# A chunked scan whose first chunks are loaded and weighed during the attention stage before it, with six state carries moved from VectorE to GpSimd

## Chip, cores and metric

One core of a Trainium2 chip runs the whole kernel as one program. The metric is device time in microseconds (us), the median of several runs. The engines are PE (TensorE), DVE (VectorE), ACT (ScalarE), POOL (GpSimd) and SP (SyncE, which here only issues DMAs). Each works through its own list of instructions in order, and they meet at semaphores.

## What is computed

One encoder layer over two request groups with shared weights, a prompt of 1024 tokens and a sample of 512: a projection, differential attention, a bidirectional Mamba-2 scan, a gated merge, routed experts, an embedding and a norm. The change lies at the seam of the attention and the scan. The scan, for one direction (it runs a second time over the flipped sequence):

```python
a = dtr * A.reshape(G, R)
acum = jnp.cumsum(a, axis=2)
xdt = xr * dtr[..., None]
...
decay_s = jnp.exp(acum[:, :, -1:] - acum)
states = jnp.einsum('bcjgn,bcjgrp->bcgrpn', Br, xdt * decay_s[..., None])
...
prev = jnp.einsum('bkcgr,bcgrpn->bkgrpn', Dm, states)
y_off = jnp.einsum('bkign,bkgrpn->bkigrp', Cr, prev) * jnp.exp(acum)[..., None]
return (y_diag + y_off).reshape(b, L, SSM_HEADS, P)
```

`states` is what one chunk of 128 tokens adds to the state, and `prev` is the state that a chunk starts from, carried over all chunks before it.

## The kernel before

The kernel is a row of stages, one function each. A stage opens a block in which every engine has its program, and the next stage's block opens when all engines have left the one before. `attend` is followed by `scan_ssm`, then `merge_branches`.

**attend** goes through 48 units (4 heads, 12 tiles of 128 queries). DVE's last work in it is `a` of the last unit (L931). POOL stores the output of a head, the last one by L862, and waits for that store to land before it leaves. SP loads the biases of the last head (L838) and then has nothing left to issue.

**scan_ssm** works on 12 chunks of 128 tokens, 0 to 7 the prompt's and 8 to 11 the sample's, in two phases.

In the first phase the chunks go upward, and each chunk c passes through four engines:
- SP loads `x_in` (a ring of four buffers) from `xb_d`: chunks 0 to 3 at the start (L1050, L1054), each later one when the states of chunk c-4 are made (L1062). Behind chunk 4's load SP waits for the flag `laid`, issues the four loads of `bst` (L1068), and only then loads chunk 5.
- DVE weighs: two TENSOR_TENSOR of 128x1024 multiply `x_in` with the broadcast `wgt` into one of two `wide` buffers (L1120, in `weigh`). From chunk 2 on it waits until the states of chunk c-2 have been made from that buffer.
- PE makes the states of both directions in PSUM (L1304), in one of two sets of banks, so it waits for the copies of chunk c-2.
- ACT copies them out: the forward half to `prev[c + 1]` (L1245), the backward half to `prev[c - 1]` (L1247).

Then the forward carry of a chunk, two TENSOR_TENSOR of 64x1024 (`carry`, L1039 and L1040): `step_ = prev[c] * rate`, `prev[c + 1] += step_`. DVE does them for chunks 1 to 6, 9 and 10, each behind the weighing of the second next chunk (`carry_on`). Beside this come fills: DVE clears four ends of `prev` (L1108), ACT clears `bst` and `mov` (L1214, L1215) before its first copy, and between copies it lays ones, head rows, sides and skips (L1221, L1227, L1232, L1238). The flag `laid` rises when the first head rows are laid.

In the second phase the chunks go downward, n = 0 for chunk 11 to n = 11 for chunk 0. PE waits for all copies, then for the count of carries, and multiplies (L1317, L1329, L1352); ACT takes exponentials (L1263, L1267, L1271), DVE multiplies and gates (L1156, L1160, L1151, L1171), and POOL adds up the squares of a finished chunk in a tree of three additions (L1203, L1204, L1207). The backward carries stay on DVE in this phase.

Of the kernel before, what the change touches and what calls it, by code (L numbers as in the profile page):

```python
# [18 lines left out]
P = 128  # L19
D = 1024  # L20
# [758 lines left out]
def attend(nc, qkT_d, v_d, line_d, ident, raw, q_hi, q_lo, k_hi, k_lo, bias0, lam, o_ssq, o_d, g_out):  # L779
# [14 lines left out]
    with ExitStack() as ctx:  # L794
        sb = lambda n, s, d=F32: ctx.enter_context(nc.sbuf_tensor("at_" + n, s, d))
        sem = stage_semaphores(nc, ctx, "at_")
        idn = sb("idn", [P, P])
# [12 lines left out]
        consts_in = sem("consts_in")  # L810
# [93 lines left out]
        @block.vector  # L904
        def _(dve):
            for k in range(NU + 1):
                if k < NU:
                    head, g0, b, L = UNITS[k]
                    hs = head % 2
                    if k % PER == 0 and head:  # L910
                        dve.wait_ge(bias_landed[hs], 32 * (P // REP) * ((head + 1) // 2))
                    at = (T1 - P) - b * P
                    if k >= 2:
                        dve.wait_ge(mixed, k - 1)
                    dve.wait_ge(sc_full, k + 1)
# [66 lines left out]
def scan_ssm(nc, xb_d, bcT_d, wgt, etot, zgT_d, d_skip, tri_d, ident, decay_d, yT_d, var_d):  # L982
# [14 lines left out]
    with ExitStack() as ctx:  # L997
        sb = lambda n, s, d=F32: ctx.enter_context(nc.sbuf_tensor("sc_" + n, s, d))
        sem = stage_semaphores(nc, ctx, "sc_")
        tri, ones, idn, idr = sb("tri", [P, 4, P]), sb("ones", [P, P]), sb("idn", [P, P]), sb("idr", [P, P], F32R)  # L1000
        far, pick = sb("far", [P, 2, P], F32R), sb("pick", [P, H])
        dsk = sb("dsk", [P, H])
        x_in = sb("x_in", [P, XR, D + P])
        wide = sb("wide", [P, 2, H, P])
# [31 lines left out]
        def carry(eng, chain, d, c, to):  # L1036
# [8 lines left out]
        carried_f = [c for c in range(NC) if c not in FIRST and c not in LAST]  # L1045
# [3 lines left out]
        def _(sp):  # L1049
            sp.dma_start(x_in[:, 0], xb_d[0][:, 0:D + P]).then_inc(x_landed[0], 16)  # L1050
            for out, src in ((idn[:], ident), (dsk[:], d_skip.to_broadcast([P, H])), (tri[:], tri_d)):
                sp.dma_start(out, src).then_inc(consts_in, 16)
            for c in range(1, XR):
                sp.dma_start(x_in[:, c], xb_d[c][:, 0:D + P]).then_inc(x_landed[c], 16)  # L1054
# [49 lines left out]
        def _(dve):  # L1104
            dve.memset(ones[:], 1.0)
            for d, zeros in ((0, FIRST), (1, LAST)):
                for c in zeros:
                    last = dve.memset(prev[side(d), c], 0.0)  # L1108
            last.then_inc(ones_set, 1)
            r = Chain(dve, carry_step)  # L1110

            def weigh(chunk):
                r, s = chunk % XR, chunk % 2
                dve.wait_ge(x_landed[r], 16 * (chunk // XR + 1))
                if chunk >= 2:
                    dve.wait_ge(st_full, chunk - 1)
                xw = flat(wide[:, s])
                for d in range(2):
                    w = wgt[:, chunk, d * H:(d + 1) * H].unsqueeze(2).to_broadcast([P, H, SP_])
                    last = dve.tensor_tensor(heads(xw[:, d * D:(d + 1) * D]), heads(x_in[:, r, 0:D]), w, ALU.mult)  # L1120
                last.then_inc(spread, 1)

            weigh(0)
            dve.wait_ge(consts_in, 48)
# [4 lines left out]
            weigh(1)  # L1129
# [47 lines left out]
            for n in range(NC):  # L1177
# [7 lines left out]
                if c in carried_b:  # L1185
                    carry(dve, r, 1, c, c - 1)
# [12 lines left out]
        def _(pool):  # L1199
            t = Chain(pool, tree)  # L1200
# [10 lines left out]
        def _(act):  # L1211
            act.preload_act_table(ACT.Exp)
            act.wait_ge(ones_set, 1)
            act.activation(bst[:].rearrange("p c d j -> p (c d j)"), ones[:, 0:1].to_broadcast([P, NC * 2 * P]), ACT.Copy, scale=0.0).then_inc(zeroed, 1)  # L1214
            act.activation(mov[:].rearrange("p s i -> p (s i)"), ones[:, 0:1].to_broadcast([P, 2 * H * P]), ACT.Copy, scale=0.0).then_inc(zeroed, 1)  # L1215

            def lay_rates():
                act.wait_ge(zeroed, 2)
# [4 lines left out]
            def lay_heads(s):  # L1223
                act.wait_ge(picked, 1)
# [5 lines left out]
            def lay_sides():  # L1230
                act.wait_ge(consts_in, 48)
# [9 lines left out]
            for c in range(NC):  # L1241
# [54 lines left out]
        def _(pe):  # L1296
# [74 lines left out]
            pe.wait_ge(carry_step, 2 * len(carried_f))  # L1371
            for n in range(NC):
# [1079 lines left out]
def encoder_layer(nc, x, p, table, g_mix, w_in, taps, dt_bias, a_log, d_skip, g_ssm_norm, lam_params, g_subln, w_att_up, w_ssm_up, w_gate, b_gate, w_out, g_ffn, w_router, w_exp_gate, w_exp_up, w_exp_down, w_ple_gate, b_ple_gate, w_ple_proj, g_final, ident, tri, one_hot, token_ids, slot_numbers, y_prompt, y_sample):  # L2452
# [17 lines left out]
    with nc.sbuf_tensor("wgt", [P, TT, 2 * SH], F32) as wgt, nc.sbuf_tensor("etot", [P, TT, 2 * SH], F32) as etot, ExitStack() as first_head:  # L2470
# [78 lines left out]
```

## Time and profile before

| | us |
|---|---|
| median of 3 runs (2978.16 to 2982.34) | 2980.89 |
| the profiled execution | 2978.14 |
| its span, first to last instruction | 2976.5 |
| first phase of the scan in it, first instruction to last copy | 1092.17 to 1150.26 |
| second phase in it, to about | 1320 |

The profile is one execution. A row of the order of time has the start, the duration, engine, line, operation, out<-in, shapes and count; a bracket at its end gives the idle time of that engine before the row, and who ended it. Durations printed beside a count are those of the whole run of merged instructions. PE's granted clock has two levels, 1.2 GHz (0.5) and 2.4 GHz (1.0).

### The profile page before, as it was taken

The numbers are of one execution on the slowest core, as the hardware profiler recorded it, in microseconds if no ns is written. First come the engines' busy times: TensorE is split into PE (matmuls) and PEld (weight loads), VectorE is DVE, ScalarE is ACT, GpSimd is POOL, SyncE is SP. The second block draws the span as 40 slices with busy tenths as digits, with TensorE's granted clock in tenths as the row PEclk, the third lists the DMA queues.
The fourth block names the chain that finished last, engine by engine and source line by source line (L and its number), as shares of the span: only waits on it lengthen the run. The fifth ranks groups of instructions, "written<-read, shape, count | busy, mean of one in ns | idle before, by whom it ended". The sixth has DMA issues, their size and how long they took to land. (4 is left out here: it accounts for less than half of the span.)

```text
span 2976.5 us, 40939 instructions
## 1 busy us (share of the span) xinstructions
PE 2715.6 (91%) x15360; PEld 2328.1 (78%) x15360; DVE 1551.8 (52%) x2035; ACT 1297.1 (44%) x1810; POOL 315.8 (11%) x298
## 2 busy tenths in 40 slices
PE   5999999999988867967998968799999999999798
PEld 4889888788877744746887857799999999999686
DVE  5000000170127768866762247577777776776555
ACT  4111111142238876554442123455555555555445
POOL 1000000010002100220110011011111001001022
PEclk7999999999999989988999976899999999999899
DMA  4422211274332223447775542788778878878532
GB/s 147 105 71 74 103 71 58 88 236 148 105 109 70 70 81 111 127 143 226 246 249 185 198 170 75 237 243 260 239 247 252 248 238 250 256 231 245 177 148 82
DMA packets 417577, 492.36 MB, mean 165 GB/s; under 512 B 17848, under 2 KB 363976, under 8 KB 416472
## 3 DMA queue, kind: packets, MB, share of 16 engines
q1 hardware_dynamic: 391472, 386.76, 41.3%
q0 software_dynamic: 26000, 104.18, 11.0%
q8 instruction: 68, 1.11, 0.2%
q14 instruction: 37, 0.30, 0.0%
HBM read 381.64 MB, written 109.25 MB: 165 GB/s over the span
## 5 line engine op out<-in xcount | busy, mean ns | idle before, releaser
L2157 DVE TENSOR_TENSOR ex_w_lo<-ex_w_raw,ex_w_hi 128x2048 fp32r<-128x2048 f32 x195 | 444.0, 2291 | 143.0 <-ACT ex_w_hi L2114 143.0
L2246 PE MATMUL ex_ps_u<-ex_x,ex_w_hi 128*128 128x384 f32 x2048 | 411.6, 342 | 5.1 <-DVE ex_w_lo L2157 5.1
L2114 ACT ACTIVATE ex_w_hi<-ex_w_raw 128x2048 fp32r<-128x2048 f32 x195 | 370.5, 1909 | 0.8
L2246 PEld LDWEIGHTS ex_ps_u<-ex_x,ex_w_hi 128*128 128x128 f32 x2048 | 349.2, 189 | 6.2 <-issue 5.5
L2246 PEld LDWEIGHTS ex_ps_u<-ex_x,ex_w_lo 128*128 128x128 f32 x2048 | 266.2, 191 | 0.6
L2265 PE MATMUL ex_ps_d<-ex_w_hi,ex_h 128*128 128x512 f32 x768 | 266.0, 400 | 0.0
L2246 PE MATMUL ex_ps_u<-ex_x,ex_w_lo 128*128 128x192 f32 x2048 | 265.9, 273 | 0.0
L358 DVE TENSOR_TENSOR w_lo<-w_raw,w_hi 128x2048 fp32r<-128x2048 f32 x14 | 32.1, 2293 | 404.1 <-ACT w_hi L324 404.1
L330 ACT ACTIVATE stage<-ps 128x512 f32<-128x512 f32 (+1 forms) x102 | 55.8, 548 | 401.1 <-PE ps L382 345.6
L2265 PE MATMUL ex_ps_d<-ex_w_lo,ex_h 128*128 128x512 f32 x512 | 202.8, 396 | 0.0
L2265 PEld LDWEIGHTS ex_ps_d<-ex_w_hi,ex_h 128*128 128x128 f32 x768 | 144.6, 188 | 35.1
L2131 ACT ACTIVATE ex_beside<-ex_ps_u 128x384 f32<-128x384 f32 x128 | 62.9, 492 | 249.4 <-PE ex_ps_u L2246 249.4
L382 PE MATMUL ps<-u_hi,w_hi 128*128 128x512 f32 x624 | 155.9, 392 | 3.2 <-PEq L409 3.2
L382 PE MATMUL ps<-u_hi,w_lo 128*128 128x512 f32 x624 | 154.2, 389 | 0.0
L382 PE MATMUL ps<-u_lo,w_hi 128*128 128x512 f32 x624 | 154.1, 389 | 0.0
L382 PEld LDWEIGHTS ps<-u_hi,w_hi 128*128 128x128 f32 x624 | 118.1, 190 | 28.1 <-PEq L409 3.6
L382 PEld LDWEIGHTS ps<-u_hi,w_lo 128*128 128x128 f32 x624 | 117.4, 188 | 24.4
L382 PEld LDWEIGHTS ps<-u_lo,w_hi 128*128 128x128 f32 x624 | 117.1, 188 | 24.3
L2102 POOL DMA_INDIRECT h_d<-ex_y,ex_idx_out x32 | 58.3, 1823 | 689.2 <-DVE ex_y L2212 684.3
L2265 PEld LDWEIGHTS ex_ps_d<-ex_w_lo,ex_h 128*128 128x128 f32 x512 | 96.6, 189 | 22.1
L883 ACT ACTIVATE at_S<-at_S,at_low 128x1024 f32<-128x1024 f32 (+1 forms) x96 | 96.2, 1004 | 35.9 <-DVE at_low L917 35.9
L1803 PE MATMUL ou_ps_h<-half_hi,o_lo 128*128 128x512 f32 x384 | 99.6, 403 | 5.5 <-SPq L1700 5.5
(395 smaller groups left out, 4900.2 us busy)
## 6 DMA issues: line engine op xcount, KB each, us to landing
ex_w_raw<-in_w_exp_gate SPq DMA_DIRECT2D x64, 1024.0 KB, 8.0
ex_w_raw<-in_w_exp_up SPq DMA_DIRECT2D x64, 1024.0 KB, 6.3
ex_w_raw<-in_w_exp_down SPq DMA_DIRECT2D x64, 1024.0 KB, 6.8
w_raw<-in_w_in SPq DMA_DIRECT2D x15, 1024.0 KB, 5.5
g_d<-gst SPq DMA_DIRECT2D x48, 256.0 KB, 2.0
mg_w_raw<-in_w_ssm_up SPq DMA_DIRECT2D x24, 512.0 KB, 5.2
mg_g_raw<-g_d SPq DMA_DIRECT2D x24, 512.0 KB, 7.2
gw_raw<-in_w_gate SPq DMA_DIRECT2D x16, 512.0 KB, 5.4
```

The source lines that it names most:

```text
L330: act.activation(stage[:, s, j * n:(j + 1) * n], ps[:, j % RING, 0:n], func).then_inc(ps_free, 1)
L358: dve.tensor_tensor(w_lo[:, s, :, 0:n], w_raw[:, s, :, 0:n], w_hi[:, s, :, 0:n].bitcast(F32), ALU.subtract).then_inc(w_split, 1)
L382: last = pe.matmul(ps[:, j % RING, :], w[:, s, k, m * P:(m + 1) * P], v[:, k, b * BLK:(b + 1) * BLK], start=i == 0, stop=i == len(terms) - 1)
L883: act.activation(S[:, k % 2, m, 0:L], S[:, k % 2, m, 0:L], ACT.Exp, bias=low[:, k % 2, m:m + 1], scale=-1.0, accum_out=tot[:, k % 2, m:m + ...
L1803: last = pe.matmul(ps_h[:, s, c * BLK:(c + 1) * BLK], v[s][:, k], w[:, 1 - c, k], start=i == 0, stop=i == len(terms) - 1)
L2102: pool.indirect_dma_start(out=h_d, out_offset=bass.IndirectOffsetOnAxis(ap=idx_out[0:cap, g:g + 1], axis=0), in_=y[0:cap, g], in_offset=No ...
L2114: act.activation(unit(w_hi, j), w_raw[:, j % RAW], ACT.Copy).then_inc(w_hi_done, 1)
L2131: act.activation(beside[:, j % 2], ps_u[:, j % 2, :, C:2 * C], ACT.Copy).then_inc(beside_done, 1)
L2157: dve.tensor_tensor(unit(w_lo, j), w_raw[:, j % RAW], unit(w_hi, j).bitcast(F32), ALU.subtract).then_inc(w_split, 1)
L2246: last = pe.matmul(ps_u[:, j % 2, m, 0:wide * C], w[:, s // 2, k, s % 2, cols], x[:, k, 0:wide].rearrange("p a c -> p (a c)"), start=i == ...
L2265: last = pe.matmul(ps_d[:, g].rearrange("p (a c) -> p a c", a=2), *terms[i], start=i == 0, stop=i == len(terms) - 1)
```

## The change

- SP loads `x_in` of chunks 0 to 3, `dsk` and `tri` in `attend`, behind the last head's biases; `idn` is shared by both stages.
- DVE weighs chunks 0 and 1 at the end of its program in `attend` (`weigh_chunk`).
- The four clearings of `prev` go from DVE to POOL. ACT clears `bst` behind its copy of chunk 0 and `mov` behind its copies of chunk 1, and what it lays between copies comes one chunk later.
- The forward carries of chunks 1 to 6 (the prompt's) go from DVE to POOL (`early_f`), with half of `y2[:, 1]` as scratch. DVE keeps those of chunks 9 and 10. PE waits for POOL's carries before n = 4, and ACT waits for them before it writes `y2[:, 1]` (`square(1)`).

```diff
+def weigh_chunk(dve, x_in, wide, wgt, x_landed, spread, chunk):
+    r, s = chunk % 4, chunk % 2
+    dve.wait_ge(x_landed[r], 16 * (chunk // 4 + 1))
+    for d in range(2):
+        w = wgt[:, chunk, d * SH:(d + 1) * SH].unsqueeze(2).to_broadcast([P, SH, SP_])
+        x = x_in[:, r, 0:D].rearrange("p (h e) -> p h e", e=SP_)
+        last = dve.tensor_tensor(wide[:, s].rearrange("p h i -> p (h i)")[:, d * D:(d + 1) * D].rearrange("p (h e) -> p h e", e=SP_), x, w, ALU.mult)
+    last.then_inc(spread, 1)
...
+            for c in range(4):
+                sp.dma_start(x_in[:, c], xb_d[c][:, 0:D + P]).then_inc(x_landed[c], 16)
+            for out, src in ((dsk[:], d_skip.to_broadcast([P, SH])), (tri[:], tri_d)):
+                sp.dma_start(out, src).then_inc(tri_dsk_in, 16)
...
+            for chunk in range(2):
+                weigh_chunk(dve, x_in, wide, wgt, x_landed, spread, chunk)
...
-        carried_f = [c for c in range(NC) if c not in FIRST and c not in LAST]
+        carried_f = [c for c in range(TT1, NC) if c not in FIRST and c not in LAST]
+        early_f = [c for c in range(TT1) if c not in FIRST and c not in LAST]
...
         @block.gpsimd
         def _(pool):
+            for d, zeros in ((0, FIRST), (1, LAST)):
+                for c in zeros:
+                    pool.memset(prev[side(d), c], 0.0).then_inc(prev_set, 1)
+            early = Chain(pool, carried_early)
+            for chunk in early_f:
+                pool.wait_ge(kept, kept_f(chunk))
+                carry(pool, early, 0, chunk, chunk + 1, flat(y2[:, 1]))
...
                 if c == 0:
+                    zero(bst[:].rearrange("p c d j -> p (c d j)"))
                     lay_rates()
+                if c == 1:
+                    zero(mov[:].rearrange("p s i -> p (s i)"))
                     lay_heads(0)
-                if c == 1:
+                if c == 2:
                     lay_heads(1)
-                if c == 2:
+                if c == 3:
                     lay_sides()
-                if 3 <= c < 7:
-                    scale_skip(4 * (c - 3), 4 * (c - 2))
+                if 4 <= c < 8:
+                    scale_skip(4 * (c - 4), 4 * (c - 3))
...
                 act.wait_ge(y_read, 2 * n + 2)
+                if n == 1:
+                    act.wait_ge(carried_early, 2 * len(early_f))
...
                 if q == 0:
+                    if n == NC - TT1:
+                        pe.wait_ge(carried_early, 2 * len(early_f))
```

DVE before, from the last product of the attention (L931) over the seam into the scan:

```order
L931 SCALAR_TENSOR_TENSOR at_a<-at_S,at_ratio 128x512
...
L1105 MEMSET sc_ones 128x128
L1108 MEMSET sc_prev 64x1024 x4
L1120 TENSOR_TENSOR sc_wide<-sc_x_in,wgt 128x1024 x2
L1127 TENSOR_TENSOR sc_pick<-sc_idn 32x16 x2
L1120 TENSOR_TENSOR sc_wide<-sc_x_in,wgt 128x1024 x2
L1131 TENSOR_SCALAR sc_far<-sc_tri 128x128 x2
L1120 TENSOR_TENSOR sc_wide<-sc_x_in,wgt 128x1024 x4
L1039 TENSOR_TENSOR sc_step_<-sc_prev,etot 64x1024
L1040 TENSOR_TENSOR sc_prev<-sc_prev,sc_step_ 64x1024
L1120 TENSOR_TENSOR sc_wide<-sc_x_in,wgt 128x1024 x2
```

The same place in the changed kernel (L785 is the weighing, L943 the attention's last product, L1050 and L1051 the two steps of a carry):

```order
L943 SCALAR_TENSOR_TENSOR at_a<-at_S,at_ratio 128x512
L785 TENSOR_TENSOR wide<-x_in,wgt 128x1024 x4
...
L1112 MEMSET sc_ones 128x128
L1124 TENSOR_TENSOR sc_pick<-idn 32x16 x2
L1127 TENSOR_SCALAR sc_far<-tri 128x128 x2
L785 TENSOR_TENSOR wide<-x_in,wgt 128x1024 x20
L1050 TENSOR_TENSOR sc_step_<-sc_prev,etot 64x1024
L1051 TENSOR_TENSOR sc_prev<-sc_prev,sc_step_ 64x1024
```

Two chunks are weighed ahead of the seam, the other ten stand in one row of 20 instructions, and no carry of the prompt is left between them.

POOL before, from the last store of the attention to the first tree of squares in the scan:

```order
L862 DMA o_d<-at_o 128x12x128 x2
...
L1203 TENSOR_TENSOR sc_y24<-sc_y2 128x512
L1204 TENSOR_TENSOR sc_y22<-sc_y24 128x256
L1207 TENSOR_TENSOR sc_y2s<-sc_y22 128x128
```

POOL in the changed kernel, the same place:

```order
L874 DMA o_d<-at_o 128x12x128 x2
...
L1198 MEMSET sc_prev 64x1024 x4
L1050 TENSOR_TENSOR sc_y2<-sc_prev,etot 64x1024
L1051 TENSOR_TENSOR sc_prev<-sc_prev,sc_y2 64x1024
...
L1206 TENSOR_TENSOR sc_y24<-sc_y2 128x512
L1207 TENSOR_TENSOR sc_y22<-sc_y24 128x256
L1210 TENSOR_TENSOR sc_y2s<-sc_y22 128x128
```

POOL had nothing to do in the first phase and now has four clearings and six pairs like the one shown, ahead of the first tree.

ACT before, from the first instruction of the scan:

```order
L1214 ACTIVATE sc_bst<-sc_ones 128x3072
L1215 ACTIVATE sc_mov<-sc_ones 128x4096
L1245 ACTIVATE sc_prev<-sc_ps 64x1024
L1221 ACTIVATE sc_bst<-sc_ones 2x12x128 x2
L1227 ACTIVATE sc_mov<-sc_pick 32x2048 x2
L1245 ACTIVATE sc_prev<-sc_ps 64x1024
L1247 ACTIVATE sc_prev<-sc_ps 64x1024
```

ACT in the changed kernel:

```order
L1251 ACTIVATE sc_prev<-sc_ps 64x1024
L1219 ACTIVATE sc_bst<-sc_ones 128x3072
L1225 ACTIVATE sc_bst<-sc_ones 2x12x128 x2
L1251 ACTIVATE sc_prev<-sc_ps 64x1024
L1253 ACTIVATE sc_prev<-sc_ps 64x1024
L1219 ACTIVATE sc_mov<-sc_ones 128x4096
L1232 ACTIVATE sc_mov<-sc_pick 32x2048 x2
```

The first copy moves ahead of both clearings; the laying of the head rows (L1227, now L1232), which raises `laid`, stays behind both.

## Rows read from the trace of the kernel before

**Rows 1.** First phase: us, busy PE, PEld, DVE, ACT, POOL; clock, DMA share, GB/s
```profile
1092.00:1150.30 58.30, 32.16 (x96) 7.83 (x96) 49.75 (x48) 43.92 (x47) 0.00 (x0) 0.74 0.52 162
```
**Rows 2.** Order of time, end of the attention: start, us, engine, line, what
```profile
988.76 4.11 SPq L838 DMA_DIRECT2D at_bias<-line_d  x8
...
1081.10 0.75 DVE L931 SCALAR_TENSOR_TENSOR at_a<-at_S,at_ratio 128x512 f32<-128x512 f32 x1
...
1086.79 1.02 POOL L862 DMA_DIRECT2D o_d<-at_o  x1 [36.41 <-ACT at_o L902]
1092.17 0.34 SPq L1050 DMA_DIRECT2D sc_x_in<-xb_d  x1
```
**Rows 3.** Order of time, start of the scan
```profile
1092.17 1.28 ACT L1212 ACT_TABLE_LOAD   x1 [5.68 <-PEq L794]
...
1092.59 0.91 DVE L1108 MEMSET sc_prev<- 64x1024 f32 x1 [0.15 <-issue]
...
1096.84 2.36 DVE L1120 TENSOR_TENSOR sc_wide<-sc_x_in,wgt 128x1024 f32<-128x1024 f32 x2
1096.85 2.76 ACT L1214 ACTIVATE sc_bst<-sc_ones 128x3072 fp32r<-128x3072 f32 x1 [3.39 <-DVE sc_prev L1108]
...
1099.26 3.68 PE L1304 MATMUL sc_ps<-sc_wide,sc_x_in 128*64 128x512 f32 x8 [13.52 <-DVE sc_wide L1120]
1099.52 3.60 ACT L1215 ACTIVATE sc_mov<-sc_ones 128x4096 fp32r<-128x4096 f32 x1
...
1103.02 1.00 ACT L1245 ACTIVATE sc_prev<-sc_ps 64x1024 f32<-64x1024 f32 x1
...
1107.03 3.82 ACT L1227 ACTIVATE sc_mov<-sc_pick 32x2048 fp32r<-32x2048 f32 x2
```
**Rows 4.** Order of time, the first phase's middle
```profile
1110.88 1.77 SPq L1068 DMA_DIRECT2D sc_bst<-decay_d  x4
...
1111.93 1.22 DVE L1039 TENSOR_TENSOR sc_step_<-sc_prev,etot 64x1024 f32<-64x1024 f32 x1 [3.32 <-ACT sc_prev L1245]
...
1122.78 1.94 PE L1304 MATMUL sc_ps<-sc_wide,sc_x_in 128*64 128x512 f32 x8 [0.23 <-DVE sc_wide L1120]
...
1125.14 2.36 DVE L1120 TENSOR_TENSOR sc_wide<-sc_x_in,wgt 128x1024 f32<-128x1024 f32 x2
...
1128.66 1.22 DVE L1040 TENSOR_TENSOR sc_prev<-sc_prev,sc_step_ 64x1024 f32<-64x1024 f32 x1
```
**Rows 5.** Issue to landing of chunk 5's load, issued at 1112.69
```profile
DMA to landing us min/median/max: 4.2/4.2/4.2
```
**Rows 6.** Order of time, end of the first phase
```profile
1148.32 1.94 ACT L1247 ACTIVATE sc_prev<-sc_ps 64x1024 f32<-64x1024 f32 x2
...
1150.86 1.22 DVE L1040 TENSOR_TENSOR sc_prev<-sc_prev,sc_step_ 64x1024 f32<-64x1024 f32 x1
...
1152.99 0.69 DVE L1156 TENSOR_TENSOR sc_E<-sc_E,sc_Eb 128x512 f32<-128x512 f32 x1 [0.92 <-ACT sc_Eb L1267]
```
**Rows 7.** Order of time, POOL's first tree with DVE beside it, second phase
```profile
1174.35 1.77 POOL L1203 TENSOR_TENSOR sc_y<-sc_y 128x512 f32<-128x512 f32 x1 [86.53 <-ACT sc_y L1283]
1176.20 1.07 POOL L1204 TENSOR_TENSOR sc_y<-sc_y 128x256 f32<-128x256 f32 x1
...
1175.50 1.17 DVE L1156 TENSOR_TENSOR sc_E<-sc_E,sc_Eb 128x512 f32<-128x512 f32 x1
1176.71 1.11 DVE L1160 TENSOR_TENSOR sc_E<-sc_E,sc_cbs 128x512 f32<-128x512 f32 x1
1177.74 0.94 DVE L1151 TENSOR_TENSOR sc_wide<-sc_ea,sc_C 128x512 f32<-128x512 f32 x1
```
**Rows 8.** Order of time, POOL's last tree, DVE idle beside it
```profile
1316.92 1.26 POOL L1203 TENSOR_TENSOR sc_y<-sc_y 128x512 f32<-128x512 f32 x1 [4.11 <-ACT sc_y L1283]
1318.26 0.72 POOL L1204 TENSOR_TENSOR sc_y<-sc_y 128x256 f32<-128x256 f32 x1
1319.06 0.45 POOL L1207 TENSOR_TENSOR sc_y2s<-sc_y 128x128 f32<-128x128 f32 x1
```

More of the change, by code:

```diff
@@ L954, in _ @@
                     if j == 0:
-                        pe.wait_ge(consts_in, 16)
+                        pe.wait_ge(idn_in, 16)
                     if j:
@@ L999, in scan_ssm @@
         sem = stage_semaphores(nc, ctx, "sc_")
-        tri, ones, idn, idr = sb("tri", [P, 4, P]), sb("ones", [P, P]), sb("idn", [P, P]), sb("idr", [P, P], F32R)
+        ones, idr = sb("ones", [P, P]), sb("idr", [P, P], F32R)
         far, pick = sb("far", [P, 2, P], F32R), sb("pick", [P, H])
-        dsk = sb("dsk", [P, H])
-        x_in = sb("x_in", [P, XR, D + P])
-        wide = sb("wide", [P, 2, H, P])
         prev, step_ = sb("prev", [P, NC, D]), sb("step_", [P, D])
@@ L1015, in scan_ssm @@
         ps = ctx.enter_context(nc.psum_tensor("sc_ps", [P, 8, BLK], F32))
-        consts_in, ones_set, far_made, idr_made = sem("consts_in"), sem("ones_set"), sem("far_made"), sem("idr_made")
+        ones_set, prev_set, far_made, idr_made = sem("ones_set"), sem("prev_set"), sem("far_made"), sem("idr_made")
         picked, laid, bst_in, skip_made, sel_in = sem("picked"), sem("laid"), sem("bst_in"), sem("skip_made"), sem("sel_in")
-        x_landed = [sem("x_landed%d" % r) for r in range(XR)]
-        spread, st_full, kept, carry_step = sem("spread"), sem("st_full"), sem("kept"), sem("carry_step")
+        st_full, kept, carry_step = sem("st_full"), sem("kept"), sem("carry_step")
+        carried_early = sem("carried_early")
         bc_in, mv_in, z_in = ([sem(n + "0"), sem(n + "1")] for n in ("bc_in", "mv_in", "z_in"))
@@ L1034, in scan_ssm, with carry @@
         a_hi_d, a_lo_d, b_hi_d, b_lo_d = (decay_d[i] for i in range(4))
-        def carry(eng, chain, d, c, to):
+        def carry(eng, chain, d, c, to, step_):
             rate = etot[side(d), c, d * H:(d + 1) * H].unsqueeze(2).to_broadcast([SN, H, SP_])
@@ L1049, in _ @@
         def _(sp):
[L1050 to L1054, printed above, removed]
             for a, b in ((0, 2 * H), (BOTH, P)):
@@ L1104, in _ @@
         def _(dve):
[L1105 to L1109, printed above, removed]
+            dve.memset(ones[:], 1.0).then_inc(ones_set, 1)
             r = Chain(dve, carry_step)
             def weigh(chunk):
-                r, s = chunk % XR, chunk % 2
-                dve.wait_ge(x_landed[r], 16 * (chunk // XR + 1))
                 if chunk >= 2:
                     dve.wait_ge(st_full, chunk - 1)
[L1117 to L1124, printed above, removed]
+                weigh_chunk(dve, x_in, wide, wgt, x_landed, spread, chunk)
+            dve.wait_ge(idn_in, 16)
+            dve.wait_ge(consts_in, 32)
             for d in range(2):
@@ L1135, in carry_on @@
                     dve.wait_ge(kept, kept_f(chunk))
-                    carry(dve, r, 0, chunk, chunk + 1)
+                    carry(dve, r, 0, chunk, chunk + 1, step_)
             for chunk in range(2, NC):
@@ L1185, in _ @@
                 if c in carried_b:
-                    carry(dve, r, 1, c, c - 1)
+                    carry(dve, r, 1, c, c - 1, step_)
                 decays_times_cb(n, 2)
@@ L1213, in _, with zero @@
             act.wait_ge(ones_set, 1)
-            act.activation(bst[:].rearrange("p c d j -> p (c d j)"), ones[:, 0:1].to_broadcast([P, NC * 2 * P]), ACT.Copy, scale=0.0).then_inc(zeroed, 1)
-            act.activation(mov[:].rearrange("p s i -> p (s i)"), ones[:, 0:1].to_broadcast([P, 2 * H * P]), ACT.Copy, scale=0.0).then_inc(zeroed, 1)
+            def zero(out):
+                act.activation(out, ones[:, 0:1].to_broadcast([P, out.shape[-1]]), ACT.Copy, scale=0.0).then_inc(zeroed, 1)
             def lay_rates():
-                act.wait_ge(zeroed, 2)
+                act.wait_ge(zeroed, 1)
                 for d in range(2):
@@ L1223, in lay_heads @@
             def lay_heads(s):
+                act.wait_ge(zeroed, 2)
                 act.wait_ge(picked, 1)
@@ L1230, in lay_sides @@
             def lay_sides():
-                act.wait_ge(consts_in, 48)
+                act.wait_ge(idn_in, 16)
+                act.wait_ge(consts_in, 32)
                 act.activation(idr[:], idn[:], ACT.Copy).then_inc(idr_made, 1)
@@ L1371, in _ @@
             pe.wait_ge(carry_step, 2 * len(carried_f))
+            pe.wait_ge(prev_set, 4)
             for n in range(NC):
@@ L2489, in encoder_layer @@
                 finish_gates(nc, u_hi_now, u_lo_now, w_gate, gate_tiles, gw_raw, gw_hi, gw_lo, gst, g_out, g, tiles(qkT), line, lam_params, raw, *operands, bias0, lam)
-        attend(nc, tiles(qkT), v, line, ident, raw, *operands, bias0, lam, o_ssq, o, g_out)
+        scan_front = ExitStack()
+        near = lambda n, s: scan_front.enter_context(nc.sbuf_tensor(n, s, F32))
+        x_in, wide = near("x_in", [P, 4, D + P]), near("wide", [P, 2, SH, P])
+        idn, tri4, dsk = near("idn", [P, P]), near("tri4", [P, 4, P]), near("dsk", [P, SH])
+        idn_in, consts_in, spread = (nc.alloc_semaphore(n) for n in ("idn_in", "tri_dsk_in", "x_spread"))
+        x_landed = [nc.alloc_semaphore("x_landed%d" % c) for c in range(4)]
+        attend(nc, tiles(qkT), v, line, ident, raw, *operands, bias0, lam, o_ssq, o, g_out, tiles(xb), d_skip, tri, wgt, x_in, wide, idn, tri4, dsk, idn_in, consts_in, x_landed, spread)
         first_head.close()
-        scan_ssm(nc, tiles(xb), bcT, wgt, etot, zgT, d_skip, tri, ident, decay, yT, var)
+        scan_ssm(nc, tiles(xb), bcT, wgt, etot, zgT, tri, decay, yT, var, x_in, wide, idn, tri4, dsk, idn_in, consts_in, x_landed, spread)
+        scan_front.close()
+        DONE_WITH.extend([idn_in, consts_in, spread] + x_landed)
     tiles_of = lambda d: d.rearrange("b (i p) c -> (b i) p c", p=P)
```

9 lines of the change are left out of this document (3 added, 6 removed).

## The prediction

> **What bounds the kernel now.** I read the busy time by stretch first, then the order of time around the seam and through the scan's first phase. In that phase, 58.3 us long, DVE is busy 49.75 us, ACT 43.92, PE 32.16 at a mean granted clock of 0.74, and POOL nothing [rows 1]. So DVE sets the pace, with ACT not far behind. A middle chunk shows it: its two weighing instructions take 2.36 us, 1.18 each, its carry another two of some 1.22, and PE, which makes the chunk's states in 1.94 us at the high level of its clock, waits for DVE [rows 4]. The phase ends at 1150.26 with ACT's last two copies. DVE finishes its last carry at 1152.08 and then waits 0.92 us for ACT's exponential [rows 6], which hangs on PE and so on the copies. What counts is therefore the end of the copies: whatever moves that moves the second phase, which the change leaves as it is, and the end of the kernel with it.
>
> The start of the phase is slack. DVE clears and weighs until 1099.2, and PE begins at 1099.26 after 13.52 us of idling. ACT sits 3.39 us behind DVE's four clearings and then clears two tiles itself, so that the first copy comes at 1103.02 [rows 3].
>
> **The change part by part.** The sum is made on the profiled execution, 2978.14 us, 2.75 below the median of the runs, 2980.89; I add its differences to the median.
>
> *Loads and weighing in the attention: hidden, at no cost there.* SP has issued the last biases by 992.9, and DVE needs the first chunk only when its last product ends, at 1081.85 [rows 2]; that leaves 89 us for four loads of the kind that took 4.2 us to land [rows 5]. The four weighing instructions take 4 x 1.18 = 4.7 us and end at 1086.6. The cover is the last store of the attention: POOL issues it only at 1086.79, and the scan opens at 1092.17 [rows 2]. Without that cover the cost would be at most 4.7 us.
>
> *An earlier start.* PE can begin at about 1092.3 and at the low level of its clock has chunk 0's states 3.68 us later [rows 3], at 1096.0, where before they were there at 1102.9. DVE weighs chunks 2, 3 and 4 as fast as PE frees the buffers, by about 1104.
>
> *The flag `laid`: no earlier.* ACT's first copy now comes at 1096.0, but both clearings come after it. By the durations of [rows 3]: copy 1.0, clearing 2.76, laying of ones 3.0 (between the copy's end, 1104.02, and 1107.03), two copies 2.0, clearing 3.60, head rows 3.82, which makes 1112.2. Before it was 1110.85. Behind the flag SP issues 1.77 us of other loads [rows 4], and chunk 5's load lands 4.2 us later [rows 5]: 1118.2. So DVE, done with chunk 4 at 1104, idles for 14 us. The head start is used up there; what is left of it is that three chunks more are weighed.
>
> *The carries on POOL.* Twelve instructions of 64x1024 leave DVE, 12 x 1.22 = 14.6 us. The trace of before has no such instruction on POOL. The nearest rows are its additions with DVE idle: 0.45, 0.72 and 1.26 us for 128, 256 and 512 columns [rows 8], that is 0.54 us for 256 more, and so 1.26 + 2 x 0.54 = 2.34 us for 1024. The lower bound is DVE's own 1.22 for the same shape [rows 4]; the upper is twice 1.77, the 512 columns beside a busy DVE [rows 7], 3.54, which already holds a wait for DVE. I take 2.34, since it comes from undisturbed rows of the same operation.
>
> *What POOL costs DVE.* This decides. In POOL's first tree [rows 7] DVE's instructions of 128x512, 0.69 us undisturbed [rows 6], take 1.17, 1.11 and 0.94, and POOL's take 1.77, 1.07 and 0.79 for 1.26, 0.72 and 0.45. The ends tell how. POOL's first addition ends at 1176.12 and DVE's instruction 0.55 later, at 1176.67; POOL's next ends 0.60 after that, at 1177.27, and DVE's next again 0.55 after, at 1177.82; POOL's third 0.31 after, at 1178.13, and DVE's 0.55 after that, at 1178.68. Each ends one undisturbed working time after the other: they take turns, one instruction each, and neither runs while the other does. The weighing reads two tiles in SBUF as these DVE instructions do, and a carry on POOL reads two tiles as the additions do, so I let them take turns as well.
>
> The Trainium skill has this as a rule (SBUF — State Buffer, Who interferes with whom): a VectorE instruction with two inputs in SBUF and a GpSimd instruction that reads SBUF contend for a shared port pair, and the later one blocks until the other is done. It speaks against this change, and the trace agrees with it in the ends just read. By the rule the time is the forecast below, 2987.9; if the two only slowed each other in part it would be 2978.0, the second rival.
>
> *The sum.* Carries 1 and 2, four of POOL's instructions, fall into DVE's idle time before 1118.2 (their copies are there at about 1103.7 and 1113.2, by the walk above) and cost nothing. From then on POOL has 8 instructions and DVE the weighing of chunks 5 to 11, 14 instructions. Taking turns: 14 x 1.18 + 8 x 2.34 = 16.5 + 18.7 = 35.2 us, and the last weighing ends at 1153.4. Behind it PE makes the states, 1.94 us at the high level [rows 4] or 3.68 at the low one [rows 3], and ACT copies, 1.0: 1156.3 to 1158.1. Against 1150.26 that is 6.1 to 7.8 us later. I take the middle, 7.0, because PE has both levels in the phase before. So 2978.14 + 7.0 = 2985.1 for such an execution and 2980.89 + 7.0 = **2987.9** for the median.
>
> *Edits at nothing.* DVE's carries of chunks 9 and 10, 4 x 1.22 = 4.9 us, end at about 1158.3, and the exponential that DVE needs comes 2.7 us behind the last copy, as before [rows 6]; that hides them. POOL's clearings are over before its first carry at 1103.7, and who needs them waits for the copies anyway. Behind ACT's new wait in `square(1)` stand its exponentials, and behind those PE; but POOL ends its carries at about 1118.2 + 8 x (2.34 + 1.18) = 1146.4, while before the first tree began at 1174.35 [rows 7], and `square(1)` comes a chunk after that. The wait of PE before n = 4 is later still. Even at 3.54 us an instruction POOL ends at 1156.
>
> **The rivals.** *POOL and DVE do not get in each other's way* (faster). For it: the shape is new on POOL, with half the partitions and a broadcast operand, and no row has a POOL addition beside a weighing. Against: all of [rows 7]. Then ACT is next: 1096.0 + 43.92 - 1.28 (its table load [rows 3]) = 1138.6, 11.7 us earlier; or, with PE at the low level, chunks 5 to 11 from 1120.6 at 3.68 us each and a copy, 1147.4, 2.9 earlier. Middle 7.3: 2973.6. It decides if a DVE weighing beside a POOL carry stays at 1.2 us.
>
> *They slow each other in part.* In [rows 7] DVE lost (1.17 + 1.11 + 0.94) - 3 x 0.69 = 1.15 us to additions that take POOL 2.43 us alone [rows 8], 0.47 us for each. If that share holds, the eight carries cost DVE 0.47 x 18.7 = 8.8 us in place of 18.7: 9.9 us less than the forecast, 2.9 below before, 2978.0, no change that can be measured. Against it: the same rows read end by end.
>
> *POOL is much slower on this shape.* At 3.54 us the eight cost 28.3 us, 9.6 more: 2997.5.
>
> **How the numbers follow.** About 0.2%, 6.0 us, is what a measurement of this kernel can tell from no change. Forecast 0.60, no contention 0.15, in part 0.18, much slower 0.07. The forecast's own range, with POOL's instruction between 2.0 and 2.9 us and PE at either level, is 3 to 12 us more, 2984 to 2993; some 0.38 of its 0.60 lies beyond 6.0. Slower: 0.38 + 0.07 = 0.45. Faster: most of the first rival, 0.12, and 0.02 of the second, 0.14. Within 0.2%: the rest, 0.41. The range reaches down to the middle of the first rival, 2974, and up to 13 us over before, 2994, and leaves out less than 2 in 10.
>
> **What would show it.** Right: the weighing of chunks 0 and 1 ends by 1087 in the attention and the scan still opens near 1092; `laid` rises near 1112 and DVE idles some 14 us before chunk 5; from 1118 on weighing instructions last 3 us or more wherever a carry runs on POOL, and the copies end near 1157. Wrong: weighing instructions of 1.2 us beside running carries; a carry step on POOL far from 2.3 us; a scan that opens later; PE waiting for the early carries at n = 4.

## The result and the profile after

| | before | after |
|---|---|---|
| median of 20 runs each, us | 2978.86 (2975.84 to 2982.34) | 2983.60 (2979.64 to 2988.64) |
| ratio, with its 95% interval | | 1.0015 (1.0008 to 1.0021) |
| span of the profiled execution | 2976.5 | 2982.1 |
| the scan's first instruction | 1092.17 | 1090.59 |
| first phase, from there to the last copy | 58.1 | 62.3 |
| second phase, from there to DVE's last instruction of the scan | 170.1 | 170.6 |

The kernel became 4.7 us slower: the interval leaves no doubt of the sign, but the size is below the 0.2% that the prediction took as the limit. In the profiled executions 4.2 us of it lie in the scan's first phase. The other 1.4 of the 5.6 us between the spans are a sum of three: the scan opened 1.6 us earlier here, its second phase took 0.5 more, and what follows the scan, from the next stage's first instruction on, took 1654.8 us where it took 1652.3 before. That last stretch has the same code in all ten kernels of this study and lies between 1651.9 and 1655.4 in them, and the scan opens between 1087.0 and 1093.0: such differences are scatter. So the kernels are compared below by the length of the first phase, in one profiled execution of each, and by medians where there are several runs.

The busy time of the kernel after, with the columns and in the same 58.3 us of [rows 1] (its own first phase is wider, 1090.59 to 1152.91):

```profile
1092.00:1150.30 58.30, 31.41 (x88) 7.44 (x86) 38.96 (x23) 40.51 (x44) 34.80 (x15) 0.67 0.36 115
```

DVE is busy 38.96 us with 23 instructions, where it was busy 49.75 with 48. In the mean that is 1.7 us for one, against 1.04. POOL, idle before, is busy 34.80 us. The order of time on DVE shows where these microseconds are, from the last product of the attention to the second phase, kernel after (single weighings are from narrower stretches):

```profile
1079.51 0.75 DVE L943 SCALAR_TENSOR_TENSOR at_a<-at_S,at_ratio 128x512 f32<-128x512 f32 x1
1080.18 4.62 DVE L785 TENSOR_TENSOR wide<-x_in,wgt 128x1024 f32<-128x1024 f32 x4
...
1093.98 6.90 DVE L785 TENSOR_TENSOR wide<-x_in,wgt 128x1024 f32<-128x1024 f32 x6 [1.88 <-PE sc_ps L1315]
1116.82 13.49 DVE L785 TENSOR_TENSOR wide<-x_in,wgt 128x1024 f32<-128x1024 f32 x5 [15.94 <-DMA x_in<-xb_d]
...
1120.81 3.37 DVE L785 TENSOR_TENSOR wide<-x_in,wgt 128x1024 f32<-128x1024 f32 x1
...
1124.10 2.92 DVE L785 TENSOR_TENSOR wide<-x_in,wgt 128x1024 f32<-128x1024 f32 x1
...
1126.94 3.38 DVE L785 TENSOR_TENSOR wide<-x_in,wgt 128x1024 f32<-128x1024 f32 x1
...
1147.49 2.36 DVE L785 TENSOR_TENSOR wide<-x_in,wgt 128x1024 f32<-128x1024 f32 x2 [1.51 <-PE sc_ps L1315]
...
1155.65 0.69 DVE L1152 TENSOR_TENSOR sc_E<-sc_E,sc_Eb 128x512 f32<-128x512 f32 x1 [0.92 <-ACT sc_Eb L1276]
```

The four weighings in the attention and the six at the scan's start run at 1.2 us each. Then DVE waits 15.94 us for chunk 5's load. After that the weighings take 2.92 and 3.37 us in turn, against 1.22 alone, until POOL is done. POOL in the same stretch, kernel after:

```profile
1101.83 1.89 POOL L1050 TENSOR_TENSOR sc_y<-sc_prev,etot 64x1024 f32<-64x1024 f32 x1 [6.96 <-ACT sc_prev L1251]
1103.80 2.34 POOL L1051 TENSOR_TENSOR sc_prev<-sc_prev,sc_y 64x1024 f32<-64x1024 f32 x1
1111.48 1.89 POOL L1050 TENSOR_TENSOR sc_y<-sc_prev,etot 64x1024 f32<-64x1024 f32 x1 [5.34 <-ACT sc_prev L1251]
1113.45 2.34 POOL L1051 TENSOR_TENSOR sc_prev<-sc_prev,sc_y 64x1024 f32<-64x1024 f32 x1
...
1119.88 3.21 POOL L1051 TENSOR_TENSOR sc_prev<-sc_prev,sc_y 64x1024 f32<-64x1024 f32 x1
1123.17 2.76 POOL L1050 TENSOR_TENSOR sc_y<-sc_prev,etot 64x1024 f32<-64x1024 f32 x1
1126.01 3.22 POOL L1051 TENSOR_TENSOR sc_prev<-sc_prev,sc_y 64x1024 f32<-64x1024 f32 x1
...
1138.28 3.20 POOL L1051 TENSOR_TENSOR sc_prev<-sc_prev,sc_y 64x1024 f32<-64x1024 f32 x1
```

While DVE idles, the two steps of a carry take 1.89 us (the multiplication) and 2.34 (the addition); beside weighings 2.76 and 3.21. The ends of both engines, in one row: POOL 1123.09, DVE 1124.18, POOL 1125.93, DVE 1127.02, POOL 1129.23, DVE 1130.32. Each kind of instruction ends a fixed time after the other engine's, a little less than it takes alone: 1.09 us for a weighing, 1.75 for the multiplication, 2.21 for the addition. They take turns, as the additions of the tree did in [rows 7].

ACT and SP, kernel after, from the loads in the attention to the last copy:

```profile
991.11 2.97 SPq L848 DMA_DIRECT2D x_in<-xb_d  x4
...
1094.04 1.02 ACT L1251 ACTIVATE sc_prev<-sc_ps 64x1024 f32<-64x1024 f32 x1 [2.17 <-PE sc_ps L1315]
1094.96 2.75 ACT L1219 ACTIVATE sc_bst<-sc_ones 128x3072 fp32r<-128x3072 f32 x1
...
1102.82 3.62 ACT L1219 ACTIVATE sc_mov<-sc_ones 128x4096 fp32r<-128x4096 f32 x1
1106.46 3.83 ACT L1232 ACTIVATE sc_mov<-sc_pick 32x2048 fp32r<-32x2048 f32 x2
...
1110.32 2.22 SPq L1075 DMA_DIRECT2D sc_bst<-decay_d  x4
1112.58 23.52 SPq L1069 DMA_DIRECT2D x_in<-xb_d  x7
...
1151.89 1.02 ACT L1253 ACTIVATE sc_prev<-sc_ps 64x1024 f32<-64x1024 f32 x1 [0.25 <-PE sc_ps L1315]
```

The head rows that raise `laid` end at 1110.29, 19.7 us after the scan's first instruction; before it was 18.7. Chunk 5's load is issued behind the four of `bst` at 1112.58, and DVE has it at 1116.82.

### The profile page after: what moved, and what is told of

It reads as the page before. It is cut to its first block and busy times, and to the rows that moved or that the text cites. A ratio compares the mean times of both kernels' runs of the same rounds, so it can differ in the third digit from the quotient of the medians.

```text
span 2982.1 us, 40956 instructions
## 1 busy us (share of the span) xinstructions
PE 2718.1 (91%) x15360; PEld 2328.0 (78%) x15360; DVE 1549.1 (52%) x2019; ACT 1297.5 (44%) x1810; POOL 348.5 (12%) x314
```

## The experiments

**Theory T (turns):** POOL's two-input instructions and the weighings exclude each other, and that alone is what the change costs. **Rivals:** the share of a wait (S: each microsecond of POOL takes about half a microsecond from DVE), or another part of the change (L: the loads behind `laid`, the fills moved on ACT). Phase below always means the time from the scan's first instruction to the last copy, 58.1 us before and 62.3 after.

| kernel | median, us | of before beside it | ratio (95%) | phase, us | weighings in the middle, us |
|---|---|---|---|---|---|
| carries back on DVE | 2977.05 | 2979.98 | 0.9992 (0.9984 to 1.0001) | 56.3 | 1.22 |
| loads free of `laid` | 2981.73 | 2979.98 | 1.0010 (1.0000 to 1.0019) | 59.6 | 2.92 / 3.37 |
| both | 2975.57 | 2979.98 | 0.9991 (0.9982 to 0.9999) | 55.4 | 1.22 |
| before, carries on POOL alone | 2984.94 | 2979.28 | 1.0021 (1.0012 to 1.0030) | 63.3 | 2.92 / 3.37 |
| memsets for carries | 2967.35, one run | 2979.98 | | 47.4 | 1.22 |
| one-input POOL instructions | 2970.96, one run | 2979.28 | | 52.0 | 1.21 / 2.05 |
| multiplication twice | 2987.99, one run | 2979.28 | | 70.3 | 2.92 / 3.37 |
| both, and clearings on POOL | 2968.66 | 2979.28 | 0.9964 (0.9951 to 0.9978) | 48.1 | 1.22 |

**The carries back on DVE, the rest of the change kept.**

```diff
-        carried_f = [c for c in range(TT1, NC) if c not in FIRST and c not in LAST]
+        carried_f = [c for c in range(NC) if c not in FIRST and c not in LAST]
...
-            early = Chain(pool, carried_early)
-            for chunk in early_f:
-                pool.wait_ge(kept, kept_f(chunk))
-                carry(pool, early, 0, chunk, chunk + 1, flat(y2[:, 1]))
...
```

> The changed kernel with the six carries of the prompt given back to VectorE and nothing else undone. First phase of the scan, first instruction to last copy: 58.1 us before, 62.3 after the change. Taking turns: no weighing lasts longer than 1.23 us; from chunk 5's weighing, 26.2 us into the phase, VectorE has 14 weighing instructions and the carries 3 to 6, 16.5 + 9.8 us, then 3 us for the last states and copy: about 55.5 us, 7 below the changed kernel and 2.5 below before, near 2976. Rival, the late load of chunk 5 and TensorE at its low clock are what lengthens the phase: neither is touched, the phase stays within 2 us of 62, near 2983. Rival, GpSimd and VectorE only share: 16.5 us of weighing cost some 9 us too much, which the carries' own 9.8 us on VectorE replace: no change.

The phase is 56.3 us, 6.0 shorter than after, and every weighing takes 1.2 us again. So moving the carries to POOL costs 6.0 us, and all else in the change is worth 1.8 us in the phase (58.1 to 56.3). The median's ratio, 0.9992, has an interval that reaches 1.0001: that gain can't be told from no change. DVE in this kernel, order of time:

```profile
1118.83 2.36 DVE L785 TENSOR_TENSOR wide<-x_in,wgt 128x1024 f32<-128x1024 f32 x2 [2.61 <-DMA x_in<-xb_d]
...
1137.91 4.63 DVE L785 TENSOR_TENSOR wide<-x_in,wgt 128x1024 f32<-128x1024 f32 x4
1143.90 2.36 DVE L785 TENSOR_TENSOR wide<-x_in,wgt 128x1024 f32<-128x1024 f32 x2 [1.35 <-PE sc_ps L1309]
```

These rows also bear on PE's clock as a cause: its mean granted level over the phase was 0.74 before, 0.68 after and 0.70 here, and DVE's wait for PE ahead of the last chunk is 1.35 us here and 1.51 after. PE was hardly different in the two kernels, and 6.0 us lie between them.

**The carries on POOL as the only change to the kernel before.**

```diff
...
-        carried_f = [c for c in range(NC) if c not in FIRST and c not in LAST]
+        carried_f = [c for c in range(TT1, NC) if c not in FIRST and c not in LAST]
+        early_f = [c for c in range(TT1) if c not in FIRST and c not in LAST]
...
+            early = Chain(pool, carried_early)
+            for chunk in early_f:
+                pool.wait_ge(kept, kept_f(chunk))
+                carry(pool, early, 0, chunk, chunk + 1, flat(y2[:, 1]))
...
```

> The kernel before with one part of the change alone: the prompt's six carries on GpSimd; loads, weighings and clearings stay where they were. First phase 58.1 us before. Taking turns: 65 us, 7 more, near 2986. No contention: 50 to 52, near 2973, since 14.6 us leave VectorE. Sharing in part: about 57, no change.

The phase is 63.3 us, 5.2 longer than before, where 65 was expected for turns, 57 for sharing and 52 at most for no contention. DVE and POOL in this kernel, order of time:

```profile
1112.68 4.07 DVE L1122 TENSOR_TENSOR sc_wide<-sc_x_in,wgt 128x1024 f32<-128x1024 f32 x2 [6.42 <-DMA sc_x_in<-xb_d]
1118.31 29.66 DVE L1122 TENSOR_TENSOR sc_wide<-sc_x_in,wgt 128x1024 f32<-128x1024 f32 x12 [1.55 <-PE sc_ps L1312]
...
1109.64 2.33 POOL L1041 TENSOR_TENSOR sc_prev<-sc_prev,sc_y 64x1024 f32<-64x1024 f32 x1
...
1119.04 2.76 POOL L1040 TENSOR_TENSOR sc_y<-sc_prev,etot 64x1024 f32<-64x1024 f32 x1
```

Twelve weighings take 29.66 us where twelve alone would take about 14. Only one carry falls into an idle stretch of DVE here, two in the kernel after. From both sides the carries cost 5 to 6 us.

**Chunk 5's load and the later ones no longer behind `laid`, carries left on POOL.**

```diff
-                if c == XR:
+                if c == NC - 1:
                     sp.wait_ge(laid, 1)
```

> The changed kernel with the four loads behind the flag laid moved behind the last chunk's load, so that chunk 5's load no longer waits for the flag; the carries stay on GpSimd. Taking turns: the 16 us of VectorE idling before chunk 5 go, but all 12 carry steps then run beside weighings and each blocks one: about 59.5 us, 3 below the changed kernel, still 1 above before, near 2980. Rival, the late load is the cause: the phase loses most of the 16 us and ends below 50 us, near 2970. Rival, sharing in part: about 54 us.

The phase is 59.6 us: 2.8 shorter than after, still 1.5 longer than before, and the weighings beside carries take the same 2.92 and 3.37. It agrees with the expected 59.5 by luck: DVE's idling was to go and all 12 carry steps were to hold weighings up, and neither happened. DVE in this kernel, order of time:

```profile
1109.01 2.36 DVE L785 TENSOR_TENSOR wide<-x_in,wgt 128x1024 f32<-128x1024 f32 x2 [5.12 <-PE sc_ps L1315]
1118.68 2.36 DVE L785 TENSOR_TENSOR wide<-x_in,wgt 128x1024 f32<-128x1024 f32 x2 [7.32 <-PE sc_ps L1315]
1122.87 25.16 DVE L785 TENSOR_TENSOR wide<-x_in,wgt 128x1024 f32<-128x1024 f32 x10 [1.83 <-PE sc_ps L1315]
```

DVE still waits 14.3 us in these three rows, now for PE, which waits for ACT's copies (6.00 us ahead of chunk 4's states). Carries 1 and 2 fall into this idle time as they do in the kernel after, and the first step of carry 3 is over before DVE goes on; seven steps hold weighings up, where after it was eight. What the free load brings is that chunks 5 and 6 are weighed in between, undisturbed. So the flag costs 2.8 us by holding weighings back until the carries are in their way; it is not what makes the kernel slower.

**Both edits, the carries on DVE and the loads free.** The edits are the first and the third above.

> Both edits: carries back on VectorE and chunk 5's load not behind the flag. Taking turns: VectorE works from 3.4 us into the phase without a long stop, 20 weighing instructions and the carries, and ends the phase at 52 to 54.5 us, 4 to 6 below before, near 2974; faster than both kernels. Rival, late load alone: as in the run with the load alone free, below 50 us. Rival, GpSimd's carries are a help when the load is not late: slower than the run with the load alone free.

The phase is 55.4 us, about 1 longer than the upper end of what was expected. The order of time on DVE in this kernel has the reason:

```profile
1101.88 2.36 DVE L785 TENSOR_TENSOR wide<-x_in,wgt 128x1024 f32<-128x1024 f32 x2
1108.96 1.22 DVE L1050 TENSOR_TENSOR sc_step_<-sc_prev,etot 64x1024 f32<-64x1024 f32 x1 [4.72 <-ACT sc_prev L1247]
```

With the load no longer late, DVE waits 4.72 us for ACT's copy of chunk 2, which stands behind the clearing of `mov` and the head rows, 3.62 and 3.83 us in the rows of ACT above. The next bound behind the load is ACT's fills, which I had not walked through for this kernel.

**POOL instructions that read nothing.** Each carry on POOL becomes two memsets of its shape, so the prompt's forward carries are left out.

```diff
-                carry(pool, early, 0, chunk, chunk + 1, flat(y2[:, 1]))
+                for d in range(2):
+                    early.step(pool.memset(flat(y2[:, 1])[side(0)], 0.0))
```

> The changed kernel with each of GpSimd's 12 carry steps replaced by a clearing of the same scratch, 64x1024, which reads nothing; the prompt's forward carries are left out. Same number of GpSimd instructions, same waits. Taking turns at reading: weighing instructions beside the clearings take 1.2 us, and the phase ends at 46 to 51 us, the time without contention. Rival, any GpSimd instruction holds VectorE up: weighings of 2 us and more remain. Rival, late load or low clock: 62 us as after the change.

DVE and POOL in this kernel, order of time:

```profile
1118.71 4.63 DVE L785 TENSOR_TENSOR wide<-x_in,wgt 128x1024 f32<-128x1024 f32 x4 [15.24 <-DMA x_in<-xb_d]
1124.08 7.07 DVE L785 TENSOR_TENSOR wide<-x_in,wgt 128x1024 f32<-128x1024 f32 x6 [0.74 <-PE sc_ps L1316]
...
1119.43 1.95 POOL L1203 MEMSET sc_y<- 64x1024 f32 x2 [3.99 <-ACT sc_prev L1252]
1125.43 1.95 POOL L1203 MEMSET sc_y<- 64x1024 f32 x2 [1.44 <-ACT sc_prev L1252]
```

Four weighings take 4.63 us and six 7.07 with POOL working beside them, and the phase is 47.4. What holds the weighings up is thus not that POOL works but that it reads. The 14.9 us between this phase and that of after are about the price of the turns: four multiplications at 1.75 and four additions at 2.21 make 15.8.

**POOL instructions that read one tile.** The same, with a multiplication by 1.0 in place of the memset.

```diff
-                carry(pool, early, 0, chunk, chunk + 1, flat(y2[:, 1]))
+                for d in range(2):
+                    early.step(pool.tensor_scalar(flat(y2[:, 1])[side(0)], prev[side(0), chunk], 1.0, None, ALU.mult))
```

> The changed kernel with each of GpSimd's 12 carry steps replaced by a TENSOR_SCALAR of 64x1024 that reads one tile in SBUF; the prompt's forward carries are left out. If any reading on GpSimd takes the whole turn, as the two-input steps do: weighings of 2.5 us and more, phase 60 us or longer. If one input takes only part of it, as in the attention before the change, where VectorE's product beside such an instruction of 1.49 us took 1.50 and 1.59 us for 1.28: weighings of 1.4 to 1.9 us, phase 50 to 55. If only two inputs contend: 1.2 us, phase as with clearings, 47.

DVE and POOL in this kernel, order of time:

```profile
1122.08 15.64 DVE L785 TENSOR_TENSOR wide<-x_in,wgt 128x1024 f32<-128x1024 f32 x10 [0.46 <-PE sc_ps L1316]
...
1100.37 5.62 POOL L1203 TENSOR_SCALAR sc_y<-sc_prev 64x1024 f32<-64x1024 f32 x2 [7.33 <-ACT sc_prev L1252]
...
1115.95 25.53 POOL L1203 TENSOR_SCALAR sc_y<-sc_prev 64x1024 f32<-64x1024 f32 x8 [0.32 <-ACT sc_prev L1252]
```

Every second weighing takes 2.05 us, the others 1.21, so ten take 15.64. A POOL instruction takes 2.76 us alone (5.62 for two) and 3.03 beside weighings (the median). Each of them costs DVE 2.05 - 1.22 = 0.83 us, not its own 2.76: for one input this is neither turns nor nothing. The phase lies between the two, 52.0.

**The multiplication on POOL issued twice.**

```diff
+                rate = etot[side(0), chunk, 0:H].unsqueeze(2).to_broadcast([SN, H, SP_])
+                early.step(pool.tensor_tensor(heads(flat(y2[:, 1])[side(0)]), heads(prev[side(0), chunk]), rate, ALU.mult))
                 carry(pool, early, 0, chunk, chunk + 1, flat(y2[:, 1]))
...
```

> The changed kernel with the first step of each early carry issued twice on GpSimd, the same product into the same scratch: six more instructions of 1.89 us undisturbed, four of them beside weighings. First phase 62.3 us in the changed kernel. Taking turns: each of the four holds VectorE for its whole time and brings 4 x 1.9 = 7.6 us: near 70. Sharing as read from the tree's mean slowdown, 0.47: 3.6 us, near 66. GpSimd not the cause: 62.

```profile
1113.60 39.00 DVE L785 TENSOR_TENSOR wide<-x_in,wgt 128x1024 f32<-128x1024 f32 x14 [15.95 <-DMA x_in<-xb_d]
...
1123.56 2.76 POOL L1203 TENSOR_TENSOR sc_y<-sc_prev,etot 64x1024 f32<-64x1024 f32 x1
1126.40 2.76 POOL L1050 TENSOR_TENSOR sc_y<-sc_prev,etot 64x1024 f32<-64x1024 f32 x1
1129.24 3.21 POOL L1051 TENSOR_TENSOR sc_prev<-sc_prev,sc_y 64x1024 f32<-64x1024 f32 x1
```

In these rows (the order of time on DVE and POOL in this kernel) the fourteen weighings from chunk 5 on take 39.0 us, and the phase is 70.3, 8.0 longer than after. In the kernel after the fourteen took 31.5 without a wait for PE, so four further multiplications beside the weighings cost 7.5 us, 1.9 each. That is the multiplication's whole working time, 1.89 alone, as T says; S would have the phase near 66.

**A version that beats both: the carries on DVE, the loads free, and ACT's two clearings on POOL.** Memsets didn't disturb the weighings, and ACT's fills were the bound that was left.

```diff
+            pool.memset(bst[:].rearrange("p c d j -> p (c d j)").bitcast(F32), 0.0).then_inc(zeroed, 1)
+            pool.wait_ge(zeroed, 1)
+            pool.memset(mov[:].rearrange("p s i -> p (s i)").bitcast(F32), 0.0).then_inc(zeroed, 1)
+            pool.wait_ge(zeroed, 2)
             for d, zeros in ((0, FIRST), (1, LAST)):
...
-                    zero(bst[:].rearrange("p c d j -> p (c d j)"))
...
-                    zero(mov[:].rearrange("p s i -> p (s i)"))
...
```

> Carries back on VectorE and chunk 5's load not behind the flag, as in the run with both edits (first phase 55.4 us), and the clearings of bst and mov, 2.76 and 3.6 us on ScalarE, given to GpSimd as clearings, which read nothing. Turns only where GpSimd reads: the weighings beside the clearings stay at 1.2 us, ScalarE's copies of chunks 1 and 2 come 6 us earlier, VectorE's wait of some 8 us for the copy of chunk 2 goes, and the phase ends at 47 to 50 us, 8 to 11 below before: 2968 to 2972, faster than both kernels. Rival, clearings on GpSimd hold VectorE up too: no shorter than 55.

```profile
1091.72 2.66 POOL L1196 MEMSET sc_bst<- 128x3072 f32 x1 [4.79 <-DMA o_d<-at_o]
1094.44 3.54 POOL L1198 MEMSET sc_mov<- 128x4096 f32 x1
...
1091.84 2.69 DVE L1127 TENSOR_SCALAR sc_far<-tri 128x128 fp32r<-128x128 f32 x2
1094.64 4.63 DVE L785 TENSOR_TENSOR wide<-x_in,wgt 128x1024 f32<-128x1024 f32 x4
1099.78 1.22 DVE L1050 TENSOR_TENSOR sc_step_<-sc_prev,etot 64x1024 f32<-64x1024 f32 x1 [0.51 <-ACT sc_prev L1251]
...
1105.71 1.22 DVE L1050 TENSOR_TENSOR sc_step_<-sc_prev,etot 64x1024 f32<-64x1024 f32 x1 [1.07 <-ACT sc_prev L1251]
```

By these rows of its order of time, the weighings beside POOL's clearing of `mov` take 4.63 us for four, and DVE's waits for copies are 0.51 and 1.07 us where the kernel with both edits waited 4.72. `laid` rises 13.3 us after the scan's first instruction. The phase is 48.1, and the median 2968.66, 10.6 us or 0.36% below before and 14.9 below the median of after.

## Why the prediction came out as it did

The direction and the mechanism were right: the two engines take turns, one instruction each. The median was forecast at 2987.9 and is 2983.60. Of these 4.3 us, 2.0 lie in the base (the median of before is 2978.86 over 20 runs, not 2980.89 over 3) and 2.3 in the term, +4.7 for +7.0.

**Hidden loads and weighing:** right. The weighings in the attention end at 1084.80, POOL issues the last store at 1085.20, and the scan opens 5.39 us after it, as in before (5.38).

**The flag `laid`, no earlier:** right. Forecast 20.0 us after the scan's opening, measured 19.7; chunk 5's weighing forecast at 26.0, measured 26.2. DVE idles 15.94 us there, forecast 14, because PE made the first two chunks' states in 5.02 us, where 3.68 had been taken for the first alone.

**Carries 1 and 2 free:** right, by POOL's rows at 1101.83 to 1113.45, all inside DVE's idle time.

**The sum of the turns:** the step that was mis-sized. Fourteen weighings and eight POOL steps were put at 35.2 us; from 1116.82 to the last weighing's end at 1149.85 they took 33.0, and 1.51 of that is a wait for PE. So the turns themselves made 31.5, which is 3.7 less. Two sizes are behind it. The multiplication takes 1.89 us and not 2.34: the price was drawn from additions alone [rows 8], and it holds to the digit for the carry's addition, 2.34, but a row of the multiplication did not exist and the two steps were priced alike. And a turn is shorter than the lone duration, by 0.14 for the multiplication (1.75), 0.13 for the addition (2.21) and 0.09 for the weighing (1.09 for 1.18). The ends in [rows 7] had shown as much: they lie 0.60 and 0.31 us apart for additions of 0.72 and 0.45 alone, and 0.55 for DVE's instructions of 0.69, and the prediction read each as a whole undisturbed working time. Four instructions, one of each step and two weighings, were put at 7.04 us and take 6.14 (from POOL's start at 1123.17 by the ends above, 1123.09 to 1129.23); four such rounds make 3.6 us.

**What the sum left out:** the wait for PE, 1.51 us, ahead of the last chunk's weighing. Once the carries are done, DVE weighs a chunk in 2.36 us again, and PE takes 5.77 for the states of two, at a mean granted clock of 0.63 (order of time on PE, kernel after):

```profile
1143.76 5.77 PE L1315 MATMUL sc_ps<-wide,x_in 128*64 128x512 f32 x16 [0.74 <-DVE wide L785]
```

**The tail:** 3.9 us from the last weighing to the last copy was the middle of two cases; it took 3.1. So -3.7, +1.5, -0.8 and +0.2 for the later start of chunk 5 make -2.8, the difference between +7.0 and the phase's +4.2.

**Edits at nothing:** right. DVE still waits 0.92 us for ACT's exponential at 1155.65, as in [rows 6]; POOL ends its carries at 1141.48, long before the second phase asks for them, and that phase takes 170.6 us against 170.1.

**The rivals:** without contention the phase would have been 46.4 with ACT as the bound (55.2 with PE at its low level); with memsets for the carries it is 47.4, so the rival's first price was near and only its condition was false for instructions that read. Sharing in part is wrong for two inputs (multiplication twice), and it is what one input does. The third rival, 3.54 us an instruction, holds in no row: POOL's steps beside weighings take up to 3.22 in the kernel after (3.43 with the loads free), but they hold DVE for 2.21 at most.

What stays open: why a turn is shorter than the lone duration, and what in a one-input instruction of POOL holds DVE for a third of its time. No run here takes either apart further.

## What to carry to other kernels

Before an elementwise step is moved to GpSimd to relieve VectorE, look for rows in which both run two-input instructions on SBUF at once: if their ends alternate, POOL's working time is added to DVE's, and a step that is dearer on POOL (here 4.2 us a carry for 2.4) makes the sum longer although DVE's own list gets shorter. What only writes (clearings) did not disturb such instructions, and giving it to GpSimd paid 7 us here. And price each operation by its own row: two steps of one shape differed by 0.45 us. Price a turn by the ends of both engines, not by lone durations: here it was some 0.1 us shorter.

## What the runs showed of the hardware

- **For the weighings, reading is what counts.** Beside memsets on POOL, weighings took 1.22 us; beside one-input instructions 1.21 and 2.05 in turn; beside two-input ones 2.92 and 3.37. That a write alone does not disturb them is also what the Trainium skill says (SBUF — State Buffer, Who interferes with whom), and the trace agrees. The same section of the Trainium skill calls this contention for the shared ports an exclusive lock, and says of VectorE's 2-port modes that whoever issues first has them for the whole instruction. The one-input row differs from such a lock, since a POOL instruction of 2.76 us held a weighing up by 0.83, and the measurement decides.
- **A one-input instruction was no cheaper on POOL.** 2.76 us for 64x1024 against 2.34 for the two-input addition and 1.89 for the multiplication with a broadcast operand.
- **Another kind of DVE instruction was held up beside memsets.** The two `far` TENSOR_SCALARs of 128x128 took 0.36 us with POOL idle (first row below, the order of time in the kernel with the carries alone on POOL), 0.98 beside POOL's clearing of `prev` (second row, kernel after) and 2.69 beside its clearing of `bst` (shown above), which ended at 1094.38, 0.15 us before them.

```profile
1098.24 0.36 DVE L1133 TENSOR_SCALAR sc_far<-sc_tri 128x128 fp32r<-128x128 f32 x2
```

```profile
1091.12 0.98 DVE L1127 TENSOR_SCALAR sc_far<-tri 128x128 fp32r<-128x128 f32 x2
```
